# Wider value blocks, split weight rounding in front of the post norms, and a new order in the openings of a three-layer transformer kernel

## Chip, cores and metric

The kernel runs on one core of one Trainium2 chip. The metric is the device time of one execution in microseconds (us). Three runs of the kernel before took 2750.37, 2750.61 and 2752.51 us, median 2750.61 us.

## What is computed

The input is 512 tokens of width 1024. Two "hybrid" layers are followed by a third block of another kind. A hybrid layer is

```python
def hybrid_layer(x, ...):
    h = rms_norm(x, g_mix_pre)
    u = h @ w_in                                   # 1024 -> 3200 columns
    aq, ak, av, cu, rq, rk, rv, rg = jnp.split(u, SPLITS, axis=-1)
    y_att = chunk_attention(aq, ak, av, rel_bias)  # 6 heads of 64
    y_conv = conv_module(cu, ...)                  # 31 taps, width 256
    y_ret = retention(rq, rk, rv, rg)              # 6 heads of 64
    mix = jnp.concatenate([y_att, y_conv, y_ret], axis=-1) @ w_out
    x = x + rms_norm(mix, g_mix_post)
    h = rms_norm(x, g_mlp_pre)
    f = jnp.square(jax.nn.relu(h @ w_up)) @ w_down # 1024 -> 4096 -> 1024
    return x + rms_norm(f, g_mlp_post)
```

`av` and `rv`, the values of the attention and of the retention, are 384 columns each. The third block (a gated MLP, a state space scan, two attentions, gates, a second gated MLP) begins with an RMS norm of the same kind.

## The kernel before

**Products in three passes.** Every weight and every activation of a product is split into a rounded tile (`w_hi`, `h_hi`) and a rest (`w_lo`, `h_lo`), and TensorE (PE) computes hi x hi, hi x lo and lo x hi into the same PSUM bank. Activations lie with features on the partitions: 8 tiles (`KD = 8`) of 128 x 512. The weights come in a list of pieces (`layer_pieces`, 50 for each layer), each at most 8 x 256 columns, in two slots that alternate. SyncE loads a piece into `w_raw`; ScalarE (ACT) rounds it in `round_block` (L347); VectorE (DVE) subtracts in `rest_block` (L356); PE multiplies in `product` (L387). The rounding of piece n + 2 waits until PE has finished piece n, since it overwrites that piece's `w_hi`.

**Kinds of piece.** A "feat" piece of 256 columns is two output tiles of 128 features x 512 tokens: 2 x 8 x 3 matmuls with 512 moving columns. A "tok" piece gives four tiles with tokens on the partitions; its moving operand is the weight, so each of its 4 x 8 x 3 matmuls streams as many columns as the piece is wide. The 14 pieces of `w_in` (`N_IN = 14`) are: 0 and 1 the convolution's input; 2 to 4 the attention's queries and keys; 5 and 6 its values, tok, 256 and 128 columns; 7 to 9 the retention's queries and keys; 10 and 11 its values, tok, 256 and 128 columns; 12 and 13 its gates. Then follow 4 pieces of `w_out` and 32 of the MLP.

**Attention between the products.** The 24 attention steps (head, query tile) run in slots inside pieces 8 to 13: at a slot PE makes the scores of step i (L725), turns the probabilities of step i - 2 (L736) and mixes step i - 3 with the values (L746); DVE adds the bias and takes the maximum (L1183 to L1197), ACT takes the exponential (L976) and copies the turned probabilities (L985). A feat tile of 24 matmuls has two slots, a tok tile one (`slots_of`). Six rotary steps (L717, L1149 to L1153) lie in every second slot from piece 10 on. After the attends of a piece, DVE's order has `rest_block` of the piece two further on.

**Post norm and opening.** At the end of the mixing part and of the MLP the output is normed and added to x. ACT squares the output tiles (L1060, L431); GpSimd (POOL) adds squares 1 to 5 to square 0 (`squares_added`, L453); PE sums over the partitions with a matrix of ones (`added_total`: L458 for the added tile, L436 for tiles 6 and 7, two passes each); ACT takes logarithm and exponential (`norm_rooted`, L476, L478). In `post_norm_dve` DVE scales output tile k (L487), makes the `h_lo` of tile k - 1 (L513) and adds tile k to x (L524). In `split_x` ACT makes `h_hi` of tile k from x (L508) and then the square of x (L532), and POOL adds those squares as well (L453). The next norm's root is applied later, to the products' outputs, so PE can begin on unnormed x: `opening` runs the next two pieces tile by tile in the order `OPENING`: tiles 0 to 4 of both pieces, tiles 5 to 7 of the first, the sum of squares, tiles 5 and 6 of the second, a "turn" of the root where the next layer needs one (L466), tile 7 of the second. For each tile k it waits for `h_lo` and issues, for either output tile, hi x hi (L561), hi x lo (L562), lo x hi (L563). There are six openings: the first one of the kernel (order `FIRST_OPENING`), one in front of the MLP of either layer, one at the end of either layer, and one in front of the third block's second MLP.

The rounding and the rest of the second opening piece stand, on ACT and DVE, between the last output tile and the post norm:

```python
                    act.activation(sq_f[:, k, :], tile_of(b, m), ACT.Square).then_inc(S["squares"], 1)
                    act.activation(out_sb[:, k, :], tile_of(b, m), ACT.Copy).then_inc(S["g_free"], 1)
                round_block(act, b.n + 2)
            norm_rooted(act, N0 + 1)
```

## Time and profile before

| | us |
|---|---|
| median of the runs | 2750.61 |
| the profiled execution: its own time | 2752.54 |
| its span in the trace | 2750.7 |
| PE busy in the span | 2640.1 (96%) |
| DVE busy | 1333.4 (48%) |
| ACT busy | 943.5 (34%) |
| POOL busy | 426.2 (15%) |
| mean granted clock of PE | 0.985 of full |

The chain of work that ended last is to 87% PE, to 72% the matmuls of `product`. Busy time of an engine is the union of its instructions; matmuls overlap, so their pace is read from the distance of their starts. The profiled execution took 1.93 us more than the median run, and 1.8 us of its time lie outside the span.

### The profile page before, as it was taken

Reading aid. Unit: us, or ns where it says so; the run is one execution under the profiler, and the core shown is the slowest. Engines: PE = TensorE matmul, PEld = TensorE weight load, DVE = VectorE, ACT = ScalarE, POOL = GpSimd, SP = SyncE. Lnnn points to the kernel's source line nnn. Section 1 sums busy time; section 2 is a strip of 40 time slices with the busy share of each in tenths; the row PEclk is TensorE's granted clock in tenths of the full one; section 3 lists DMA queues with packets and bytes.
Section 4 is the critical chain, followed back from the end, with each engine's and each line's share of the span. In section 5 each row is a group of like instructions: output and inputs, shape, how many; then the busy total and the mean of one; then the engine's idle time right before and its main releaser. Section 6 shows DMA issues by size and latency. Waiting matters only on the chain.

```text
span 2750.7 us, 31141 instructions
## 1 busy us (share of the span) xinstructions
PE 2640.1 (96%) x12096; PEld 2083.9 (76%) x12096; DVE 1333.4 (48%) x1649; ACT 943.5 (34%) x1340; POOL 426.2 (15%) x375
## 2 busy tenths in 40 slices
PE   8999899999999989999899999899999997999998
PEld 6875688887876668888688888777776675788886
DVE  6744542334854463243544332597864456443432
ACT  4333442332333443232332232432344453322221
POOL 2101100001110110000211101186620320111100
PEclk9999999999999999999999999999999998999999
DMA  3310222222220112223132223411231033222222
GB/s 140 134 39 31 72 97 100 99 92 92 100 85 31 60 65 105 92 92 107 61 107 91 98 101 108 150 62 61 73 107 66 16 106 140 77 104 94 84 94 82
DMA packets 41001, 241.75 MB, mean 88 GB/s; under 512 B 4800, under 2 KB 5312, under 8 KB 17984
## 3 DMA queue, kind: packets, MB, share of 16 engines
q1 hardware_dynamic: 40624, 239.24, 24.7%
q8 instruction: 73, 1.20, 0.2%
q0 software_dynamic: 272, 1.05, 0.1%
q14 instruction: 32, 0.26, 0.0%
HBM read 231.88 MB, written 8.39 MB: 87 GB/s over the span
## 4 chain that ended last, share of the span: by engine, by line
PE 87%; DVE 6%; ACT 4%; issue 2%; DMA 0%; DVEq 0%; SPq 0%; ACTq 0%
PE gemm L387 72%; ACT w_hi L347 2%; DVE x_sb L524 2%; PE score L725 1%; PE mixed L746 1%; DVE w_lo L356 1%; DVE h_lo L513 1%; PE mixed L1569 1%; PE gemm L561 1%; ACT h_hi L508 1%; PE score L1558 1%; PE gemm L562 1%; PE gemm L563 1%; PE mixed L436 1%; PE turned L736 1%
## 5 line engine op out<-in xcount | busy, mean ns | idle before, releaser
L356 DVE TENSOR_TENSOR w_lo<-w_raw,w_hi 128x2048 fp32r<-128x2048 f32 (+3 forms) x225 | 474.3, 2108 | 698.1 <-ACT w_hi L347 697.9
L387 PE MATMUL gemm<-h_hi,w_hi 128*128 128x512 f32 x1744 | 693.8, 398 | 7.6 <-DVE w_lo L356 7.2
L387 PE MATMUL gemm<-h_hi,w_lo 128*128 128x512 f32 x1744 | 681.1, 391 | 0.0
L387 PE MATMUL gemm<-h_lo,w_hi 128*128 128x512 f32 x1744 | 680.5, 390 | 0.0
L347 ACT ACTIVATE w_hi<-w_raw 128x2048 fp32r<-128x2048 f32 (+3 forms) x225 | 393.4, 1749 | 450.4 <-PE gemm L387 398.8
L387 PEld LDWEIGHTS gemm<-h_hi,w_hi 128*128 128x128 f32 x1744 | 328.6, 188 | 78.8 <-DVE w_lo L356 8.2
L387 PEld LDWEIGHTS gemm<-h_hi,w_lo 128*128 128x128 f32 x1744 | 328.2, 188 | 69.7
L387 PEld LDWEIGHTS gemm<-h_lo,w_hi 128*128 128x128 f32 x1744 | 328.7, 188 | 66.0 <-issue 1.7
L387 PE MATMUL gemm<-f_hi,w_hi 128*128 128x512 f32 x512 | 199.2, 389 | 0.0
L387 PE MATMUL gemm<-f_lo,w_hi 128*128 128x512 f32 x512 | 199.2, 389 | 0.0
L387 PE MATMUL gemm<-f_hi,w_lo 128*128 128x512 f32 x512 | 199.2, 389 | 0.0
L453 POOL TENSOR_TENSOR sq_f<-sq_f 128x512 f32<-128x512 f32 x30 | 47.7, 1589 | 742.0 <-ACT sq_f L431 648.1
L387 PE MATMUL gemm<-g_hi,w_hi 128*128 128x512 f32 x352 | 137.1, 390 | 0.0
L387 PE MATMUL gemm<-g_lo,w_hi 128*128 128x512 f32 x352 | 136.9, 389 | 0.0
L387 PE MATMUL gemm<-g_hi,w_lo 128*128 128x512 f32 x352 | 136.9, 389 | 0.0
L561 PE MATMUL gemm<-h_hi,w_hi 128*128 128x512 f32 x192 | 83.0, 432 | 43.2 <-issue 20.5
L1717 POOL TENSOR_TENSOR swi<-swi,rs 128x512 f32<-128x512 f32 x44 | 56.9, 1295 | 404.6 <-ACT swi L1825 404.6
L387 PEld LDWEIGHTS gemm<-f_hi,w_lo 128*128 128x128 f32 x512 | 96.1, 188 | 20.1
L387 PEld LDWEIGHTS gemm<-f_lo,w_hi 128*128 128x128 f32 x512 | 96.1, 188 | 19.9
L387 PEld LDWEIGHTS gemm<-f_hi,w_hi 128*128 128x128 f32 x512 | 96.1, 188 | 19.8
L387 PE MATMUL gemm<-w_hi,h_hi 128*128 128x256 f32 (+1 forms) x352 | 107.5, 305 | 0.0
L1072 ACT ACTIVATE tt<-tt 128x512 f32<-128x512 f32 x64 | 40.3, 632 | 194.1 <-DVE tt L1276 194.1
(379 smaller groups left out, 3888.2 us busy)
## 6 DMA issues: line engine op xcount, KB each, us to landing
w_raw<-in_w SPq DMA_DIRECT2D x171, 1024.0 KB, 4.7
w_raw<-in_w SPq DMA_DIRECT2D x16, 768.0 KB, 4.0
w_raw<-in_w SPq DMA_DIRECT2D x16, 640.0 KB, 3.7
w_raw<-in_w SPq DMA_DIRECT2D x18, 512.0 KB, 3.5
bias_t<-in_att_bias SPq DMA_DIRECT2D x2, 1536.0 KB, 8.8
decay_t<-in_c_decay SPq DMA_DIRECT2D x2, 1536.0 KB, 8.0
x_sb<-in_x SPq DMA_DIRECT2D x4, 512.0 KB, 6.5
x_kept<-x_sb SPq DMA_DIRECT2D x1, 2048.0 KB, 10.8
```

The source lines that it names most:

```text
L347: act.activation(w_hi[:, b.slot, 0:size], w_raw[:, b.slot, 0:size], ACT.Copy).then_inc(S["w_rounded"], 1)
L356: dve.tensor_tensor(w_lo[:, b.slot, 0:size], w_raw[:, b.slot, 0:size], w_hi[:, b.slot, 0:size].bitcast(F32), ALU.subtract).then_inc(S["w_r ...
L387: mm = pe.matmul(dst, lhs, rhs, start=b.first and k == 0 and j == 0, stop=b.last and k == b.kt - 1 and j == 2)
L436: mm = pe.matmul(o_ps[:, 0:n], ones[:], sq[:, k, :], start=k == 0, stop=k == KD - 1)
L453: pool.tensor_tensor(sq[:, 0, :], sq[:, 0, :], sq[:, k, :], ALU.add).then_inc(S["sq_added"], 1)
L508: act.activation(h_hi[:, k, :], x_sb[:, k, :], ACT.Copy, scale=gain[:, k:k + 1]).then_inc(S["norm_hi"], 1)
L513: dve.scalar_tensor_tensor(out=h_lo[:, k, :], in0=x_sb[:, k, :], scalar=gain[:, k:k + 1], in1=h_hi[:, k, :].bitcast(F32), op0=ALU.mult, op ...
L524: dve.tensor_tensor(x_sb[:, k, :], x_sb[:, k, :], out_sb[:, k, :], ALU.add).then_inc(S["x_done"], 1)
L561: pe.matmul(dst, wh[:, k, c], h_hi[:, k, :], start=k == 0, stop=False)
L562: pe.matmul(dst, wh[:, k, c], h_lo[:, k, :], start=False, stop=False)
L1072: act.activation(tt[:, 2 * j + m, :], tt[:, 2 * j + m, :], ACT.Square).then_inc(S["f_sq"], 1)
L1717: pool.tensor_tensor(swi[:, m, :], swi[:, m, :], rs[:], ALU.mult).then_inc(S["silu_r"], 1)
```

## The change

- The values of attention and retention are laid side by side in the weights (`in_columns`) and cut into three tok pieces of 256 columns: pieces 5 and 6, and piece 10. A layer has 13 pieces of `w_in` and 49 in all. The values lie in one buffer `values`; the last tile of `ret_sq` gets a place of its own. Every tok tile now has two slots, one halfway through its 24 matmuls and one behind them, so the number of slots stays 22.
- In front of the post norms the second opening piece is rounded and its rest taken in two halves of 128 columns of each tile (`round_half`, `rest_half`). The first half is done while PE computes the last output tile. At the end of the mixing part ACT's order is square 7, second half, root, copy of tile 7; DVE waits for that copy before the post norm. At the end of the MLP the squares of tiles 6 and 7 come ahead of the halves.
- The squares of x in the four openings behind a post norm are added by DVE inside `post_norm_dve`, one after each addition to x, and no longer by POOL.
- Everywhere one more square (tile 6) is added before the sum, so `added_total` has one tile fewer for PE.
- In `opening`, PE waits for `h_hi` of tile k, issues hi x hi and lo x hi (of both pieces where they stand together in the order), and then waits for `h_lo` and issues hi x lo.

```diff
-    feat(3 * a, 3 * a + 2 * CONV_W)
-    feat(0, 2 * a)
-    tok(2 * a, 3 * a)
-    r = 3 * a + 2 * CONV_W
-    feat(r, r + 2 * RET_W)
-    tok(r + 2 * RET_W, r + 3 * RET_W)
-    feat(r + 3 * RET_W, r + 4 * RET_W)
+    feat(0, 2 * CONV_W)
+    feat(QK_AT, QK_AT + 2 * a)
+    tok(VALUES_AT, VALUES_AT + 2 * WCOLS)
+    feat(RQK_AT, RQK_AT + 2 * RET_W)
+    tok(VALUES_AT + 2 * WCOLS, VALUES_AT + 3 * WCOLS)
+    feat(RG_AT, RG_AT + RET_W)
...
+        def round_half(act, n, m):
+
+            b = plan[n]
+            if m == 0:
+                act.wait_ge(w_in_s[b.slot], ONCE.loads(n))
+            act.wait_ge(S["units"], plan[n - 2].u0 + m + 1)
+            act.activation(half_of(w_hi, b, m), half_of(w_raw, b, m),
+                           ACT.Copy).then_inc(S["w_rounded"] if m else S["half_rounded"], 1)
+
+        def rest_half(dve, n, m, halves):
+
+            b = plan[n]
+            if m:
+                dve.wait_ge(S["w_rounded"], n + 1)
+            else:
+                dve.wait_ge(S["half_rounded"], halves)
+            dve.tensor_tensor(half_of(w_lo, b, m), half_of(w_raw, b, m), half_of(w_hi, b, m).bitcast(F32),
+                              ALU.subtract).then_inc(S["w_rest"] if m else S["half_rest"], 1)
...
-            for k in range(1, KD - 2):
+            for k in range(1, KD - 1):
...
-            for k in (KD - 2, KD - 1):
-                norm_add(pe, i, sq, k)
+            norm_add(pe, i, sq, KD - 1)
...
+            def add_square(k):
+
+                base = added_by(i + 1) - (KD - 2)
+                dve.wait_ge(S["squares"], KD * i + k + 1)
+                if k > 1:
+                    dve.wait_ge(S["sq_added"], base + k - 1)
+                dve.tensor_tensor(sq[:, 0, :], sq[:, 0, :], sq[:, k, :], ALU.add).then_inc(S["sq_added"], 1)
 
             for k in range(KD):
                 norm_scale(dve, i, k, out_sb, out_sb, gain)
@@ -522,6 +569,8 @@
                     raw_rest(dve, j, k - 1, next_gain)
                 dve.wait_ge(S["normed"], normed + k + 1)
                 dve.tensor_tensor(x_sb[:, k, :], x_sb[:, k, :], out_sb[:, k, :], ALU.add).then_inc(S["x_done"], 1)
+                if k > 1:
+                    add_square(k - 1)
             raw_rest(dve, j, KD - 1, next_gain)
...
-                    if k >= waited:
-                        pe.wait_ge(S["h_ready"], ready + k + 1)
-                        waited = k + 1
+                    pe.wait_ge(S["norm_hi"], ready + k + 1)
...
                         pe.matmul(dst, wh[:, k, c], h_hi[:, k, :], start=k == 0, stop=False)
-                        pe.matmul(dst, wh[:, k, c], h_lo[:, k, :], start=False, stop=False)
-                        mm = pe.matmul(dst, wl[:, k, c], h_hi[:, k, :], start=False, stop=k == KD - 1)
-                        if k == KD - 1:
-                            mm.then_inc(S["units"], 1)
+                        pe.matmul(dst, wl[:, k, c], h_hi[:, k, :], start=False, stop=False)
+                    held.append(b)
+                    if n + 1 < len(order) and order[n + 1] == (1 - at[0], k):
+                        continue
+                    pe.wait_ge(S["h_ready"], ready + k + 1)
+                    for b in held:
+                        wh = view(w_hi, b)
+                        for m in range(b.tiles):
+                            mm = pe.matmul(bank[b.bank + m][:], wh[:, k, m * P:(m + 1) * P], h_lo[:, k, :],
+                                           start=False, stop=k == KD - 1)
+                            if k == KD - 1:
+                                mm.then_inc(S["units"], 1)
+                    held = []
...
             squares_added(pool, N0 + 1, sq_f)
-            squares_added(pool, N0 + 2, out_sb)
             squares_added(pool, N0 + 3, sq_f)
-            squares_added(pool, N0 + 4, sq_f)
...
                     for m in range(b.tiles):
+                        softmax(slot0[b.i] + 2 * m)
                         if m % 2:
                             for q in (m - 1, m):
-                                evacuate_one(b, q, rv[:, q, cols])
-                        softmax(slot0[b.i] + m)
+                                evacuate_one(b, q, values[:, 2, q, :])
+                        softmax(slot0[b.i] + 2 * m + 1)
...
+                    if k == KD - 1:
+                        round_half(act, b.n + 2, 1)
+                        norm_rooted(act, N0 + 1)
                     act.activation(out_sb[:, k, :], tile_of(b, m), ACT.Copy).then_inc(S["g_free"], 1)
-                round_block(act, b.n + 2)
-            norm_rooted(act, N0 + 1)
+                    if k == KD - 2:
+                        round_half(act, b.n + 2, 0)
+                if b.i < W_OUT + 3:
+                    round_block(act, b.n + 2)
...
-            norm_squares(act, N0 + 3, out_sb, sq_f, wait=(S["g_free"], last_down), tiles=(KD - 2, KD - 1))
+            for m in range(2):
+                norm_squares(act, N0 + 3, out_sb, sq_f, wait=(S["g_free"], last_down), tiles=(KD - 2 + m,))
+                round_half(act, plan1[DOWN[1] + 7].n + 2, m)
             norm_rooted(act, N0 + 3)
...
+            for m in range(2):
+                rest_half(dve, plan1[W_OUT + 3].n + 2, m, 2 * lay + 1)
+            dve.wait_ge(S["g_free"], plan1[UP[0]].t0)
+            post_norm_dve(dve, N0 + 1, gains["mix_post"], cnt("normed", 0), J0 + 2, gains["mlp_pre"], out_sb)
```

## Rows read from the trace of the kernel before

**Rows 1.** The page: busy us of each engine, share of the span, instructions.
```profile
PE 2640.1 (96%) x12096; PEld 2083.9 (76%) x12096; DVE 1333.4 (48%) x1649; ACT 943.5 (34%) x1340; POOL 426.2 (15%) x375
```

**Rows 2.** Windows, instructions of L387 alone: both value pieces of the attention, layer 0.
```profile
72.55:84.06 11.51, 11.51 (x97) 11.51 (x96) 1.00 0.42 153
84.06:94.74 10.68, 10.68 (x99) 10.68 (x97) 1.00 0.58 225
```

**Rows 3.** Windows, all engines: the two value pieces of the retention, layer 0.
```profile
143.84:165.28 21.44, 21.44 (x140) 16.71 (x139) 10.15 (x25) 7.14 (x18) 0.27 (x1) 1.00 0.08 25
165.28:185.78 20.50, 20.50 (x140) 16.02 (x139) 11.12 (x25) 6.96 (x17) 0.00 (x0) 1.00 0.15 52
```

**Rows 4.** Chain of work, 143 to 170 us: start us, us, what.
```profile
160.51 3.05 PE gemm L387 x24
...
165.34 2.83 PE gemm L387 x24
```

**Rows 5.** Timeline of DVE, 143 to 154 us.
```profile
146.72 1.22 DVE L356 TENSOR_TENSOR w_lo<-w_raw,w_hi 128x1024 fp32r<-128x1024 f32 x1 [1.77 <-ACT w_hi L347]
147.87 0.28 DVE L1183 SCALAR_TENSOR_TENSOR probs<-score,bias_t 128x128 f32<-128x128 f32 x1
```

**Rows 6.** Timeline of ACT, 144 to 150 us.
```profile
145.65 1.04 ACT L347 ACTIVATE w_hi<-w_raw 128x1024 fp32r<-128x1024 f32 x1
```

**Rows 7.** Timeline of ACT, 305.7 to 312.5 us (end of the output projection).
```profile
305.78 0.60 ACT L1060 ACTIVATE sq_f<-gemm 128x512 f32<-128x512 f32 x1 [4.35 <-PE gemm L387]
306.27 0.59 ACT L1061 ACTIVATE out_sb<-gemm 128x512 f32<-128x512 f32 x1
306.75 1.91 ACT L347 ACTIVATE w_hi<-w_raw 128x2048 fp32r<-128x2048 f32 x1
308.55 0.69 ACT L476 ACTIVATE rs<-mixed,eps_c 128x512 f32<-128x512 f32 x1
309.27 0.63 ACT L478 ACTIVATE rs<-rs 128x512 f32<-128x512 f32 x1
```

**Rows 8.** Timeline of DVE, 305.7 to 322 us (post norm in front of the MLP).
```profile
310.90 0.74 DVE L487 SCALAR_TENSOR_TENSOR out_sb<-out_sb,par_sb,rs 128x512 f32<-128x512 f32 x1
...
313.83 0.68 DVE L524 TENSOR_TENSOR x_sb<-x_sb,out_sb 128x512 f32<-128x512 f32 x1
...
315.30 0.75 DVE L513 SCALAR_TENSOR_TENSOR h_lo<-x_sb,par_sb,h_hi 128x512 fp32r<-128x512 f32 x1
315.97 1.77 DVE L524 TENSOR_TENSOR x_sb<-x_sb,out_sb 128x512 f32<-128x512 f32 x1
```

**Rows 9.** Timeline of POOL, 311 to 322 us.
```profile
315.86 1.33 POOL L453 TENSOR_TENSOR out_sb<-out_sb 128x512 f32<-128x512 f32 x1 [18.99 <-ACT out_sb L532]
```

**Rows 10.** Chain of work, 290 to 350 us.
```profile
312.40 0.73 ACT h_hi L508
...
333.65 0.76 DVE h_lo L513
...
336.96 1.72 PE mixed L436 x4
...
342.79 7.25 PE gemm L387 x32
```

**Rows 11.** Windows, all engines: stretches of three openings (the granted clock behind the busy times).
```profile
308.30:314.00 5.70, 0.01 (x1) 0.02 (x1) 5.15 (x6) 2.81 (x5) 0.00 (x0) 0.71 0.31 92
314.00:317.50 3.50, 3.49 (x8) 2.79 (x9) 3.37 (x4) 1.24 (x2) 1.33 (x1) 0.50 0.38 157
...
2373.90:2377.60 3.70, 0.01 (x1) 0.00 (x0) 3.00 (x3) 0.74 (x2) 0.00 (x0) 1.00 0.00 0
```

**Rows 12.** Chain of work, 669 to 712 us (end of layer 0).
```profile
669.28 1.91 ACT w_hi L347
...
675.17 0.76 DVE out_sb L487
...
708.25 3.85 PE gemm L387 x17
```

More of the change, by code:

```diff
@@ L598, in slots_of @@
         def slots_of(b):
-            return 2 * b.tiles if b.kind == "feat" else b.tiles
+            return 2 * b.tiles
         slot0 = {b.i: sum(slots_of(c) for c in plan[SOFT_AT:b.i]) for b in plan[SOFT_AT:N_IN]}
@@ L779, in layer_tensor @@
                     product(pe, b, h_hi, h_lo, halfway=lambda m: attend(slot0[b.i] + 2 * m), between=after)
-                else:
-                    product(pe, b, h_hi, h_lo, between=lambda m: attend(slot0[b.i] + m))
                 if b.i == MEAN_AT:
@@ L916, in layer_gpsimd @@
             by_root(plan1[9], [rqk[:, 4 + m, :] for m in range(2)])
-            for b in plan1[12:14]:
-                by_root(b, [rg[:, 2 * (b.i - 12) + m, :] for m in range(b.tiles)])
+            for b in plan1[11:13]:
+                by_root(b, [rg[:, 2 * (b.i - 11) + m, :] for m in range(b.tiles)])
             pool.wait_ge(S["ln_done"], cnt("ln_done", 2))
```

69 lines of the change are left out of this document (42 added, 27 removed).

## The prediction

> **What bounds the kernel now.** I read the page first, then PE's idle gaps in the timeline, then the chain of waits and the windows of the stages that the change touches. PE is busy for 96% of the span [rows 1], so time can only come from two places: matmuls that go away or run at a worse pace than they need, and the few places where PE waits. The change works on one of each.
>
> The first is the value pieces. A tok tile streams the weights, so a piece of 128 columns needs as many matmuls as one of 256. The reader is to see that it is hardly quicker: 96 matmuls take 11.51 us at 256 columns, 0.120 us each, and 10.68 us at 128, 0.111 us each [rows 2]. In the retention's pieces, runs of 24 take 3.05 and 2.83 us [rows 4].
>
> The second is the openings behind a post norm. PE waits 5.7 us for the first tile [rows 11], works through the early tiles, and in the end waits for the last `h_lo`, ready at 334.4, before it can finish at 342.8 [rows 10]. DVE feeds it too slowly, and the rows show why: the addition to x takes 0.68 us while POOL rests and 1.77 us while POOL adds squares [rows 8, 9]; POOL's add begins 0.11 us ahead of DVE's. Five of the eight additions are of the slow kind. A tile then takes 1.77 - 0.08 (the overlap of neighbours) + 0.73 of ACT [rows 10] + 0.75 of DVE + handoffs, 3.24 us, where PE needs only 12 matmuls of 7.25/32 = 0.227 us [rows 10], 2.72 us.
>
> **Value pieces.** Removed for each layer: two pieces of 128 columns, 10.68 + 4 x 2.83 = 22.0 us. Added: one of 256, 11.51 us if it lies alone. The second half of piece 6 lies outside the attention, the third piece inside it, so I take piece by piece: pieces 5 and 6 go from 22.19 to 23.02 us (+0.8), and the retention's loses 4 x 2.83 = 11.3. Net -10.5 us. The attention's own matmuls stay, as does the number of slots.
>
> What this uncovers: the pieces 10 and 11 took 41.9 us for eight slots, 5.2 us each [rows 3]; now it is (41.9 - 11.3)/8 = 3.8 us. DVE has 21.3 us of work in them, less than the 30.6 that are left, so on average it keeps up. The critical place is the start of the piece. There ACT rounds and DVE takes the rest of the piece two further on, and this is now a wide one: 1.91 and 2.29 us (the wide rest is twice the 1.22 less a fixed part) instead of 1.04 and 1.22 [rows 5 to 7]. DVE's first pass over the scores slips from 147.87 to 149.9, while PE, with 12 matmuls of 0.127 us in front of a slot, is at its second slot at 149.2 (143.8, twice 12 matmuls of 3.05/24, and between them a slot's attention, on average (41.9 - 12.2 - 11.3)/8 = 2.3) and waits there for DVE to free the score bank and then for ACT's copy. A walk through the steps of the piece with the durations of the trace gives 1.5 us, once, and then DVE catches up. Bounds: nothing, and 1.5 us at each of the four tiles, 6.0. I take 1.5: -9.0 us a layer, **-18.0 us**. DMA: one load fewer and the same bytes; the loads run a piece ahead. The convolution's taps on DVE, which PE waits for behind piece 7, are spread over pieces 1 to 6 and get 0.8 us more.
>
> A rule that speaks against this part stands in the Trainium skill, TensorE: Matmul & The Clock Gate, section Back-to-back issue gap: the isolated distance of two matmuls grows with the streamed columns, N/2.4 + 2.5 ns. By it two narrow matmuls cost 112 ns and a wide one 109, and the part would gain 0.3 us a layer before the stall. The rows go against it: 0.111 and 0.120 us.
>
> **Start of the post norm.** In front of the MLP ACT does square 0.60, copy 0.59, rounding 1.91, logarithm 0.69, exponential 0.63, and DVE's rest ends only at 310.9 [rows 7, 8]. After: square (to 306.4), half a rounding (1.04 as in rows 6, to 307.3) beside PE's sum, which has two passes fewer (4 take 1.72 us [rows 10]) and ends at 307.5; logarithm, exponential, copy to 309.4; DVE's half rest (1.22) ends at 308.6 and hides. The first scaling starts at 309.4 instead of 310.9: 1.5 us. The first halves (1.04 and 1.22) lie under PE's last output tile of 5.4 us. At the end of a layer the whole rounding stands ahead of both squares [rows 12]. After: output tile 0.7, square 0.6, two passes 1.0, logarithm and exponential 1.35, so 673.0 instead of 675.2: 2.1 us.
>
> **The opening itself.** DVE per tile: addition 0.61, addition of a square 0.61, scaling 0.66, `h_lo` 0.67 as distances of starts (0.08 less than each duration [rows 8]), 2.56 us, with ACT's 0.73 hidden under the second and third. That is quicker than PE's 2.72, so DVE's work stops being the bound and PE becomes it. PE starts with `h_hi` at 309.4 + 0.74 + 0.69 + 0.72 + handoffs = 311.7. Its work: 96 matmuls x 0.227 = 21.8, the sum 1.7 instead of 2.6, and what the low clock costs. Before, PE ran 3.5 us at half clock [rows 11]; at half speed this costs 1.8 us, hidden while DVE was the bound. It is now in the open; PE rests less (4.2 instead of 5.7 us) but begins in what was the low stretch, so I take 2.0 us, with bounds of 0 and 2.9. End: 311.7 + 21.8 + 1.7 + 2.0 = 337.2 instead of 342.8: 5.5 us, twice **-11.0**. At the end of layer 0: 673.0 + 2.2 + 21.8 + 1.7 + 1.0 (the turn) + 2.0 = 701.8 instead of 708.25 [rows 12]: 6.4; at the end of layer 1, the same without the turn, 6.3: **-12.7**.
>
> What is late next: ACT's rounding of the third piece starts when the first piece's tile 7 is done, 5.8 us before the end, and with its rest takes 4.25; it stays hidden by 1.6 us. The new wait of DVE for the last copy holds only `post_norm_dve`, and is priced above.
>
> **The other openings and sums.** The first opening saves two passes, 0.9, but POOL's sixth addition (1.3) falls on DVE's rest of piece 1, for which PE waits: 0, bounds -0.9 and +1.3. The opening in front of the last MLP saves 0.9, but (0, 0)'s hi x lo moves behind the gap of 3.7 us that ends with piece 1: +0.45. There the clock was full behind 3.7 us of rest [rows 11]; 4.2 us may drop it, so again 0, bounds -0.5 and +2. The sum for the state space part gives 0.9, the last one 0.1: **-1.0**.
>
> **Sum.** -18.0 - 11.0 - 12.7 - 1.0 = -42.7 us. Against the profiled execution's 2752.54 this is 2709.8; it stood 1.9 us above the median of 2750.61, so I predict 2708.
>
> **Rivals.**
> - *Feed still too slow.* DVE keeps the old 3.24 us a tile, since each added square waits for ACT or stalls DVE like POOL did. For: DVE is near PE's pace (2.56 against 2.72). Against: without POOL the same addition takes 0.68 [rows 8]. Then an opening gains its earlier start and the shorter sum only, 2.4 in front of an MLP and 3.0 behind it, 10.8 instead of 23.7: 2721. Chance 0.11.
> - *Attention becomes the bound.* The retention's value piece keeps the 41.9 us of pieces 10 and 11, since eight slots cannot follow faster than ACT and DVE pass a step on. Against: DVE's 21.3 us and ACT's 14.1 in 41.9 [rows 3]. Layers then lose 0.8 instead of gaining 9.0: 2708 + 19.7 = 2728. Chance 0.08.
> - *Pace by columns.* A wide matmul costs as much as two narrow ones, 0.222 us: 21.3 against 21.4 us, no gain from the value pieces, 2726. Chance 0.01, as rows 2 speak against it: 0.120 us. The Trainium skill, TensorE: Matmul & The Clock Gate, section Back-to-back issue gap, is the rule by which it would come out so.
> - *The openings don't change.* DVE's wait for the copy behind the root, and `h_lo` at the end of each tile, hold PE as long as the old order did: only pieces and small sums are left, 2750.6 - 19.0 = 2732. Chance 0.04.
> - *Slower by PE's clock.* If the clock stays at 1.2 GHz through the openings, each of the 96 matmuls costs 0.2 us more: 19.2 less the 2.0 counted, four times, 69 us: 2777. It decides from 10.7 us lost per opening, which is 23 of its 25 us at the low clock. Against: rows 11 show 3.5 us low, then full. Chance 0.02. The Trainium skill (TensorE: Matmul & The Clock Gate, Part 1: The HAM clock gate) has the clock rise with sustained activity; the rows agree, 0.50 and then full.
> - About nothing gained: 0.02.
>
> **How the numbers follow.** The forecast has 0.72. Its own range: no stall and no clock loss gives 2701 (the feed's last tile then holds PE at 1.2 us less), all upper bounds but the worst stall 2715. To leave no more than 2 in 10 out the range reaches over the first rival: 2701 to 2722. A difference of 0.2% (5.5 us) is what a measurement of this kernel can tell from none. Faster is everything but the last two: 0.96; same 0.02, slower 0.02.
>
> **What would show it.** Right: no L453 beside L524, L524 at 0.69 throughout; PE without gaps from `h_hi` 0 to the end of each opening, some 25.5 us; no 128-column matmuls in L387; PE waiting about 1.5 us at the second slot of piece 10. Wrong: gaps in front of the last tiles of an opening, waits of L725 or L736 throughout piece 10, or a half clock far into the openings.

## The result and the profile after

The changed kernel took 2715.99 us, median of 4 runs (2713.98 to 2717.78), against 2750.49 us for the kernel before on the same chip: ratio 0.9875, 95% interval 0.9861 to 0.9889. A second series of the same kernel, run at the end of the study beside other runs of the kernel before, gave 2713.20 us against 2752.36, ratio 0.9856 (0.9839 to 0.9872). The change gains 34.5 us in the first series and 39.2 in the second; I had forecast 42.7 and 2708 us. The profiled execution of the first series took 2717.78 us, with a span of 2715.9. The traces below are of this one unless I say "second trace".

The page of the changed kernel, engine busy us, share of the span and instructions, answers to [rows 1]:

```profile
PE 2614.2 (96%) x11880; PEld 2063.0 (76%) x11880; DVE 1322.3 (49%) x1675; ACT 942.2 (35%) x1334; POOL 413.0 (15%) x363
```

PE has 216 matmuls fewer: 96 in either layer's value pieces, and two passes in each of twelve sums. DVE has more instructions and POOL fewer, since DVE adds the squares in four openings.

**Value pieces.** Windows of the changed kernel, the matmuls of `product` alone (start and end, us, then PE and PE's weight loads with their counts, clock, DMA share, GB/s), answer to [rows 2]:

```profile
74.38:85.91 11.53, 11.53 (x98) 11.53 (x97) 1.00 0.31 111
85.91:97.44 11.53, 11.53 (x99) 11.53 (x98) 1.00 0.65 250
```

Both pieces now cost the same 11.53 us, 0.120 us for each of 96 matmuls; the narrow one had taken 10.68. In the retention there is one value piece where two were. Behind its start PE stops twice. The timeline of that place (start us, us, engine, line, what, and in brackets the idle time before it and who ended it):

```profile
150.27 2.29 DVE L374 TENSOR_TENSOR w_lo<-w_raw,w_hi 128x2048 fp32r<-128x2048 f32 x1 [2.62 <-ACT w_hi L365]
...
152.48 0.28 DVE L1242 SCALAR_TENSOR_TENSOR probs<-score,bias_t 128x128 f32<-128x128 f32 x1
...
152.82 0.70 PE L781 MATMUL score<-qk 64*128 64x256 f32 x2 [0.60 <-DVE probs L1242]
...
154.14 0.52 PE L792 MATMUL turned<-ident_sb,probs 128*128 128x128 f32 x3 [0.62 <-ACT out_sb L1037]
```

DVE's rest of the piece, now 2.29 us long, stands in front of its pass over the scores. PE first waits 0.60 us for the score bank and then 0.62 us for ACT's copy, 1.2 us together, once in a layer. Then DVE has caught up.

**Openings.** DVE's timeline in the opening in front of layer 0's MLP shows one tile's four operations (start us, us):

```profile
319.10 0.69 DVE L564 TENSOR_TENSOR out_sb<-out_sb 128x512 f32<-128x512 f32 x1
319.70 0.75 DVE L526 SCALAR_TENSOR_TENSOR out_sb<-out_sb,par_sb,rs 128x512 f32<-128x512 f32 x1
320.37 0.75 DVE L552 SCALAR_TENSOR_TENSOR h_lo<-x_sb,par_sb,h_hi 128x512 fp32r<-128x512 f32 x1
321.03 0.69 DVE L571 TENSOR_TENSOR x_sb<-x_sb,out_sb 128x512 f32<-128x512 f32 x1
321.63 0.69 DVE L564 TENSOR_TENSOR out_sb<-out_sb 128x512 f32<-128x512 f32 x1
```

From one added square (L564) to the next are 2.53 us, where 2.56 were forecast, and the addition to x (L571) takes 0.69 us instead of the 1.77 of [rows 8]. The windows over PE's rests and what follows them (all engines' busy time with counts, granted clock, DMA share, GB/s) answer to [rows 11]:

```profile
303.93:308.17 4.24, 0.00 (x1) 0.03 (x1) 3.20 (x5) 2.62 (x5) 0.00 (x0) 0.98 0.46 149
308.17:311.60 3.43, 3.43 (x9) 2.71 (x10) 3.30 (x6) 1.67 (x3) 0.00 (x0) 0.53 0.29 122
...
957.63:963.30 5.67, 5.67 (x13) 4.44 (x14) 5.54 (x9) 2.92 (x5) 0.00 (x0) 0.50 0.20 81
2336.68:2340.85 4.17, 0.00 (x1) 0.03 (x1) 3.04 (x3) 1.22 (x2) 0.00 (x0) 0.77 0.00 0
2340.85:2345.70 4.85, 4.85 (x12) 3.80 (x13) 2.51 (x3) 2.26 (x4) 1.33 (x1) 0.50 0.61 216
```

The rest in front of the MLP is 4.24 us instead of 5.69. Behind it PE still runs at 1.2 GHz, here for 3.4 us and in layer 1 for the rest of a stretch of 6.8 us. The last two rows are new: the opening of the last MLP, where the kernel before kept 2.4 GHz, now has half the clock for 4.85 us. PE's wait in front of it does not end with the weights of the second piece, whose rest is there at 2340.10, but with DVE's addition to x behind it, which reads the bank that this piece needs:

```profile
2340.02 1.28 DVE L2491 TENSOR_TENSOR x_sb<-x_sb,gemm 128x512 f32<-128x512 f32 x2
```

**The first opening.** DVE's and POOL's timelines, and the windows of PE's wait:

```profile
19.96 3.37 DVE L374 TENSOR_TENSOR w_lo<-w_raw,w_hi 128x2048 fp32r<-128x2048 f32 x1
...
19.63 1.56 POOL L493 TENSOR_TENSOR out_sb<-out_sb 128x512 f32<-128x512 f32 x1
```

```profile
21.00:23.40 2.40, 0.03 (x2) 0.02 (x1) 2.40 (x2) 0.00 (x0) 0.18 (x1) 1.00 0.00 0
23.40:28.20 4.80, 4.80 (x14) 3.84 (x15) 1.26 (x2) 0.00 (x0) 0.00 (x0) 0.64 0.62 218
```

The rest of piece 1 takes 3.37 us beside POOL's sixth addition, where it took 2.28 before. PE stands still for 2.4 us, and 1.3 us after it goes on its clock falls to half for 3.4 us (24.66 to 28.08 us). Before, PE had no gap here.

**Where the time went.** The table is worked out from the starts of PE's instructions at fixed places of the program, in us. Stages that the table leaves out agree within 0.2 us.

| stage | before | after | second trace | difference | forecast |
|---|---|---|---|---|---|
| start to piece 5 of layer 0 | 72.55 | 74.38 | 73.20 | +1.8 / +0.7 | 0 |
| pieces 5 to 9, each layer | 71.29 | 72.16 | 72.16 | +0.9 | +0.8 |
| piece 10 to the retention's scores, each layer | 74.50 | 65.23 | 65.23 | -9.3 | -9.8 |
| retention to the norm's sum, layer 0 (not changed) | 87.24 | 90.19 | 88.59 | +2.9 / +1.3 | 0 |
| sum to first down projection, layer 0 | 102.32 | 96.63 | 97.70 | -5.7 / -4.6 | -5.5 |
| the same, layer 1 | 102.32 | 97.80 | 97.96 | -4.5 / -4.4 | -5.5 |
| last sum to the next piece 5, layer 0 | 71.71 | 65.58 | 66.20 | -6.1 / -5.5 | -6.4 |
| last sum to the next down projection, layer 1 | 255.46 | 250.00 | 250.11 | -5.5 / -5.4 | -6.3 |
| scan to the gated unit (not changed) | 445.35 | 442.60 | 442.42 | -2.8 / -2.9 | 0 |
| gated unit to the last MLP's down projection | 392.27 | 394.21 | 391.28 | +1.9 / -1.0 | 0 |

With -0.2 in front of the scan, the two columns of differences come to -34.9 and -38.8 us. The spans of the traces differ by 34.8 and 38.6 us, the medians by 34.5 and 39.2.

### The profile page after: what moved, and what is told of

Same layout as the page of the kernel before. It is cut to its first block, busy times and chain, and to the rows that moved or that the text cites. A ratio compares the mean times of both kernels' runs of the same rounds, so it can differ in the third digit from the quotient of the medians.

```text
span 2715.9 us, 30733 instructions
## 1 busy us (share of the span) xinstructions
PE 2614.2 (96%) x11880; PEld 2063.0 (76%) x11880; DVE 1322.3 (49%) x1675; ACT 942.2 (35%) x1334; POOL 413.0 (15%) x363
## 4 chain that ended last, share of the span: by engine, by line
PE 88%; DVE 5%; ACT 4%; issue 2%; POOL 1%; DMA 0%; DVEq 0%; SPq 0%; ACTq 0%; POOLq 0%
PE gemm L427 71%; PE gemm L608 2%; PE gemm L609 2%; PE gemm L617 2%; ACT w_hi L365 1%; PE score L781 1%; PE mixed L802 1%; DVE w_lo L374 1%; PE mixed L1635 1%; PE turned L792 1%; PE score L1624 1%; PE score L1679 1%; PE gemm L1738 1%; PE turned L1693 1%; DMA w_raw<-in_w 0%
## 5 line engine op out<-in xcount | busy, mean ns | idle before, releaser
L374 DVE TENSOR_TENSOR w_lo<-w_raw,w_hi 128x2048 fp32r<-128x2048 f32 (+3 forms) x219 | 466.2, 2129 | 681.1 <-ACT w_hi L365 680.8
L365 ACT ACTIVATE w_hi<-w_raw 128x2048 fp32r<-128x2048 f32 (+3 forms) x219 | 385.4, 1760 | 441.9 <-PE gemm L427 382.5
L493 POOL TENSOR_TENSOR sq_f<-sq_f 128x512 f32<-128x512 f32 x24 | 39.5, 1648 | 751.0 <-ACT sq_f L471 693.6
L1338 DVE SCALAR_TENSOR_TENSOR tt<-gemm,rs 128x512 f32<-128x512 f32 x64 | 43.7, 687 | 102.8 <-PE gemm L427 102.8
```

Source lines behind the costliest of these rows:

```text
L365: act.activation(w_hi[:, b.slot, 0:size], w_raw[:, b.slot, 0:size], ACT.Copy).then_inc(S["w_rounded"], 1)
L374: dve.tensor_tensor(w_lo[:, b.slot, 0:size], w_raw[:, b.slot, 0:size], w_hi[:, b.slot, 0:size].bitcast(F32), ALU.subtract).then_inc(S["w_r ...
L493: pool.tensor_tensor(sq[:, 0, :], sq[:, 0, :], sq[:, k, :], ALU.add).then_inc(S["sq_added"], 1)
L1338: dve.scalar_tensor_tensor(out=tt[:, 2 * j + m, :], in0=tile_of(b, m), scalar=0.0, in1=rs[:], op0=ALU.max, op1=ALU.mult).then_inc(S["g_fre ...
```

## Experiments

Eleven kernels ran. Each ratio is to the kernel before, run on the same chip in the same series.

### The two parts alone

`values_alone` is the kernel before with the edits to the pieces and their buffers only; `openings_alone` is the changed kernel without them.

```diff
-    tok(2 * a, 3 * a)
+    tok(VALUES_AT, VALUES_AT + 2 * WCOLS)
...
-    tok(r + 2 * RET_W, r + 3 * RET_W)
+    tok(VALUES_AT + 2 * WCOLS, VALUES_AT + 3 * WCOLS)
```

> The kernel before with the value pieces alone: three wide pieces in place of four, openings, norms and sums as they were. My theory: each layer loses the retention's two narrow pieces and gains one wide one inside the attention, with a stall of about 1.5 us at the second slot of it. By the trace of the changed kernel this is 0.8 us up to piece 7 and 9.3 us down from there to the retention's scores, so 17 us in two layers: 2733.5 us. Rival 1, pace by columns: nothing, 2750. Rival 2, the clock gives a part of it back (in the changed kernel the stretches at half clock in layer 0's retention took 3 us more than before): 2736. Both parts of the change are independent if this run and the next together lose as much as the change, 34.5 us, within 3 us.

> The changed kernel with its value pieces as before: four pieces, narrow ones for the retention. All else of the change stands: DVE adds the squares, halves, the early root, the order of the openings, six additions in place of five. My theory: what the trace of the changed kernel shows outside the attention, first opening +1.8, the openings in front of the MLPs -5.7 and -4.5, behind them -6.1 and -5.5, state space -0.2, last sum -0.9, which makes -21 us: 2729.5, with 3 us either way for stretches at half clock that fall elsewhere. Rival, the openings gain what I forecast and the shortfall of the changed kernel lies in how its two parts meet: -24.7, so 2726.

Measured: 2733.20 us (0.9937, 0.9921 to 0.9954) and 2732.36 us (0.9932, 0.9915 to 0.9948), against 2750.75 before: -17.5 and -18.4 us, together -35.9, where the two series of the whole change give -34.5 and -39.2. So the parts are independent as far as 3 us can tell. Pace by columns is ruled out: the value pieces alone gain 17.5 us. In the trace the pieces 5 to 9 take 0.9 us more and the stage from piece 10 to the scores 9.3 us less, in both layers, as in the changed kernel. The openings alone gain less than I had read off the first trace (21), and in the trace the stages of the four openings lose 4.5, 5.4, 5.7 and 6.2 us, 21.8 in all, with the first at +0.4, the end of the last at +1.9, and both layers' retention behind its scores, which no edit touches, at +1.5 each, and the scan at -3.0.

### POOL adds the squares again

```diff
-                if k > 1:
-                    add_square(k - 1)
...
             squares_added(pool, N0 + 1, sq_f)
+            squares_added(pool, N0 + 2, out_sb)
             squares_added(pool, N0 + 3, sq_f)
+            squares_added(pool, N0 + 4, sq_f)
```

> The changed kernel, but POOL adds the squares in the four openings behind a post norm again and DVE doesn't; starts, order of the matmuls and pieces as changed. My theory (DVE's feed was the bound): the additions to x that fall on POOL's take 1.77 us instead of 0.69, a tile takes 3.2 instead of 2.55 us, PE waits in front of the late tiles, and an opening ends 3.1 us later in front of an MLP and 3.4 behind it: 2716 + 13 = 2729. Rival 1, the old order of the matmuls and the late start were the bound and not the feed: within 2 us of 2716. Rival 2, PE waits so much that its clock falls again within the openings: 2735 or more.

Measured: 2727.65 us (0.9907, 0.9890 to 0.9923), 11.7 more than the changed kernel's first series. DVE's and POOL's timelines of this kernel:

```profile
312.51 1.78 DVE L563 TENSOR_TENSOR x_sb<-x_sb,out_sb 128x512 f32<-128x512 f32 x1
...
315.76 1.78 DVE L563 TENSOR_TENSOR x_sb<-x_sb,out_sb 128x512 f32<-128x512 f32 x1
...
312.41 1.33 POOL L493 TENSOR_TENSOR out_sb<-out_sb 128x512 f32<-128x512 f32 x1 [1.91 <-ACT out_sb L571]
```

The addition to x takes 1.78 us again, POOL's begins 0.10 us ahead of it, and a tile takes 315.76 - 312.51 = 3.25 us. From first to last matmul the four openings take 28.65, 29.84, 28.66 and 28.62 us, as in the kernel before (28.39, 29.58, 28.38, 28.37), though they start as early as in the changed kernel. PE now waits 0.74 and 1.56 us in front of two late tiles, where the changed kernel has no gap. So what set the length of an opening was DVE's feed, and the rows show what slowed it: not that POOL had work, but that it ran beside a DVE instruction with two inputs in SBUF. The Trainium skill (SBUF — State Buffer, section Who interferes with whom) says that such an instruction contends with one of GpSimd that reads SBUF, and that issue order decides who blocks; by that rule, the rows agree, 1.78 against 0.69 us.

### The root and the rounding in their old places

```diff
-                        round_half(act, b.n + 2, 1)
-                        norm_rooted(act, N0 + 1)
...
+                round_block(act, b.n + 2)
+            norm_rooted(act, N0 + 1)
```

and the same at the end of a layer, with DVE's rest whole.

> The changed kernel with one part undone: the last piece in front of a post norm is rounded as a whole, in the old places (in front of the logarithm before an MLP, in front of the squares behind it), and DVE's rest is whole. My theory: the first scaling starts 1.5 us later in front of an MLP and 2.1 us behind it, and PE has no slack to take it up: 2716 + 7.2 = 2723. Rival 1, DVE's feed has slack over PE's pace, so a late start is partly made up: 2719. Rival 2, the longer rest (5.8 us instead of 4.2) lengthens the half clock in each opening from 3.4 to 6.8 us where it isn't so already, another 1.7 us in two of four: 2727.

Measured: 2730.92 us (0.9927, 0.9911 to 0.9944), 14.9 more: a miss, twice the forecast. The timeline of the end of layer 0 shows why:

```profile
658.84 1.91 ACT L365 ACTIVATE w_hi<-w_raw 128x2048 fp32r<-128x2048 f32 x1 [7.92 <-PE gemm L405]
660.66 1.13 ACT L449 ACTIVATE sq_f<-out_sb 128x512 f32<-128x512 f32 x2
660.78 2.29 DVE L374 TENSOR_TENSOR w_lo<-w_raw,w_hi 128x2048 fp32r<-128x2048 f32 x1 [1.31 <-ACT w_hi L365]
661.35 2.85 POOL L471 TENSOR_TENSOR sq_f<-sq_f 128x512 f32<-128x512 f32 x1 [6.56 <-ACT sq_f L449]
664.25 2.08 PE L476 MATMUL mixed<-sq_f,ones_sb 128*128 128x512 f32 x2 [5.50 <-POOL sq_f L471]
```

With the whole rounding ahead of both squares, POOL's sixth addition comes behind square 6 and beside DVE's rest, takes 2.85 us instead of 1.3, and PE's sum waits for it; then its four passes run at half the clock (2.08 us for two, against 1.02 in the changed kernel). In front of the MLPs the opening starts 1.4 us later, as forecast, but is 0.6 us shorter in layer 1 (25.48 against 26.09 us). Not DVE's slack is the reason: the stretch at half clock is 6.8 us in both, and more of it now lies in PE's rest, which leaves 4.5 us instead of 5.7 in the opening. Layer 0 follows the same measure: 25.5 us with 4.5 us of half clock here, 24.9 with 3.2 in the first trace of the changed kernel, 26.0 with 5.5 in the second.

`late_root_five` is this kernel with five additions in each sum, as before the change:

```diff
-            for k in range(1, KD - 1):
+            for k in range(1, KD - 2):
...
-            norm_add(pe, i, sq, KD - 1)
+            for k in (KD - 2, KD - 1):
+                norm_add(pe, i, sq, k)
```

> The kernel with the late root (2730.9 us, 15 more than the changed kernel, where I expected 7), and with five additions of squares in place of six in every sum, as before the change: PE takes square 6 itself. My theory: with the whole rounding in front of them both squares come late at the end of a layer, and the sixth addition, 2.85 us beside DVE's rest, lands in the open between the square and PE's sum; with five it is gone, so the end of a layer is 3.5 us shorter less 0.9 for PE's two passes, twice, while the sums elsewhere take 0.9 more: 2730.9 - 5.2 + 2.6 = 2728, and from the last down projection to the next layer it takes 3 us more than in the changed kernel instead of 7. Rival, the late root costs 7 us there whoever adds the square: 2733.

Measured: 2725.01 us (0.9904, 0.9889 to 0.9919). From the first down projection to the next layer's piece 5 it takes 329.5 us, against 333.8 with six additions and 326.7 in the changed kernel (second trace 327.3): 2.8 more, 3 expected. So the sixth addition and the halved rounding aren't two separate gains. At the end of a layer the sixth addition is only free because the halves let the square of tile 6 go ahead of the rounding; without them it costs 4.3 us, the half clock of the sum included.

### The order of the matmuls

```diff
-                        pe.matmul(dst, wl[:, k, c], h_hi[:, k, :], start=False, stop=False)
+                        pe.matmul(dst, wh[:, k, c], h_lo[:, k, :], start=False, stop=False)
+                        mm = pe.matmul(dst, wl[:, k, c], h_hi[:, k, :], start=False, stop=k == KD - 1)
...
```

The wait for `h_lo` stands in front of each tile's matmuls again.

> The changed kernel with the old order of the matmuls in all openings: hi x hi, hi x lo, lo x hi for each tile, and no start before h_lo. My theory: the order lets PE start 0.75 us earlier in the four openings behind a post norm, and in the first; the feed's end changes little, and ahead of the last MLP the six matmuls of (0, 0) lie in front of the wait again (3.7 us as before instead of 4.17), where the clock may stay up: 2716 + 4 x 0.75 + 0.7 - 2.8 (the last MLP's opening) = 2717. Rival 1, the order is what keeps PE fed with every tile, h_lo being late each time: 2722. Rival 2, the order is worth nothing: 2713.

Measured: 2715.19 us (0.9871, 0.9854 to 0.9887), 0.8 below the first series of the changed kernel and 2.0 above the second, so no difference that the medians can tell. The terms are there, though: the four openings start 0.78 us later behind the sum (5.02 us of rest against 4.24), and are 0.2 to 0.7 us shorter than in the second trace. The last MLP's opening takes 28.9 us against 29.4 and 30.0, because (0, 0)'s product with `h_lo` stands in front of the wait again, 3.72 us against 4.17, and only 3.4 us of half clock follow. What the order gains in four openings, 1.4 us by these numbers, the last one gives back in part, and the rest is below what a median tells.

### PE kept busy

```diff
+        FILL = 14
...
+                    kept_busy(pe, plan1[first.i:first.i + 2], FILL)
                     opening(pe, plan1[first.i:first.i + 2], N0 + 2, out_sb, cnt("h_ready", 2 * KD))
...
+            for j in range(n):
+                m = j % b.tiles
+                pe.matmul(bank[b.bank + m][:], view(w_hi, b)[:, j % KD, m * P:(m + 1) * P],
+                          w_hi[:, b.slot, 0:SEQ], start=True, stop=True)
```

> The changed kernel with 14 idle matmuls of 512 columns behind the norm's sum, before each of the four openings that follow a post norm. They multiply weight tiles already rounded into a bank that the opening's first matmul clears, so nothing of the result hangs on them, and at 0.227 us each they lie inside PE's rest of 4.2 us. My theory: the stretches at half clock in the openings come from that rest; without it they go (3.4, 3.4, 6.8 and 6.8 us long, so 10 us at most), but DVE's feed, 2.55 us a tile, holds PE back from 2.72, so an opening gains 1.2 to 2.5 us: 2716 - 7 = 2709, and no stretch at half clock in the four openings. Rival 1, the half clock doesn't come from the rest: stretches stay and the time is 2716. Rival 2, DVE is the bound as soon as the clock is full: 2713, with gaps of PE in front of the tiles.

Measured: 2706.88 us (0.9835, 0.9819 to 0.9852), 9.1 below the first series of the changed kernel and 6.3 below the second. Windows of this kernel, layer 0 in front of the MLP: the last matmuls before the rest and the idle ones, the first 3.4 us of the opening, and all of it:

```profile
297.70:303.10 5.40, 4.36 (x18) 2.99 (x18) 3.49 (x5) 3.55 (x6) 0.00 (x0) 1.00 0.40 118
303.10:306.50 3.40, 3.40 (x15) 2.80 (x16) 3.27 (x6) 1.60 (x4) 0.00 (x0) 1.00 0.29 120
303.10:328.00 24.90, 24.61 (x104) 19.32 (x105) 20.70 (x30) 13.64 (x21) 0.00 (x0) 1.00 0.06 21
```

The idle matmuls leave 1.04 us of rest, and the clock stays at 1.00, in all four openings. Three of them now take 24.01 us and the one with the turn 25.21, against 24.9 to 26.2 and 26.2 to 26.9 in the changed kernel's two traces. So the half clock cost 0.9 to 2.2 us an opening. 0.3 us of PE's wait is left in the middle, the first place where DVE's feed shows. The half clock does come from the rest: with all but 1.04 us of it filled, no opening has any.

### The first opening

`late_rest` lets PE take piece 1's two products with rounded weights before DVE's rest of that piece is there; `five_first` gives square 6 of this sum back to PE.

```diff
-            (1, 0), (1, 1), (0, 6), (0, 7), "sum", (1, 2), (1, 3), (1, 4), "turn", (1, 5), (1, 6), (1, 7)]
+            ("hi", 0), ("hi", 1), (0, 6), (0, 7), ("lo", 0), ("lo", 1), "sum", (1, 2), (1, 3), (1, 4), "turn",
+            (1, 5), (1, 6), (1, 7)]
```

> The changed kernel with another order in the first opening alone: for the first two tiles of piece 1 PE takes both products of the rounded weights first, for which it doesn't need DVE's rest of the piece, and the product with the rest four steps later. My theory (PE waits 2.38 us there, since POOL's sixth addition stretches DVE's rest from 2.29 to 3.37 us and PE comes 1.2 us earlier than before): the wait goes but for about 0.3 us, and the half clock behind it (24.7 to 28.1 us, 1.7 us lost) too: 2716 - 3.8 = 2712. Rival 1, the half clock is due in any case: 2714. Rival 2, the wait moves to the last tiles, whose rests DVE makes behind the piece's: 2715.5.

```diff
-            for k in range(1, KD - 1):
+            for k in range(1, KD - 1 if i > 1 else KD - 2):
...
-            norm_add(pe, i, sq, KD - 1)
+            for k in (KD - 2, KD - 1) if i == 1 else (KD - 1,):
+                norm_add(pe, i, sq, k)
```

> The changed kernel with POOL's sixth addition undone in the first opening alone (PE takes square 6 itself there, two passes, 0.43 us each). My theory (the sixth addition lies on DVE's rest of piece 1): the rest takes 2.29 us instead of 3.37, PE's wait for it becomes 1.2 instead of 2.4 us and leaves the clock at full, PE pays 0.86: in the first opening 1.1 + 1.7 - 0.9 = 1.9 us less, 2714. Rival 1, the half clock stays: 2715.8, no change. Rival 2, DVE's rest is slow for another reason (it waits or takes 3.37 with POOL at rest too): 2717.

Measured: 2710.22 us (0.9852, 0.9835 to 0.9868) and 2713.13 us (0.9860, 0.9844 to 0.9875). In `late_rest` PE has no gap in the opening, the clock stays at 1.00, and piece 5 starts at 70.96, 3.4 us earlier than in the first trace of the changed kernel and 2.2 earlier than in the second. DVE's timeline of `five_first`, and the window of PE's wait in it:

```profile
20.00 2.28 DVE L374 TENSOR_TENSOR w_lo<-w_raw,w_hi 128x2048 fp32r<-128x2048 f32 x1
```

```profile
21.14:22.33 1.19, 0.00 (x1) 0.00 (x1) 1.19 (x2) 0.00 (x0) 0.00 (x0) 1.00 0.00 0
22.33:28.50 6.17, 6.17 (x26) 4.96 (x27) 1.27 (x2) 0.34 (x1) 0.00 (x0) 1.00 0.48 170
```

Without POOL's sixth addition the rest takes 2.28 us instead of 3.37, and the wait is 1.19 us instead of 2.4: the cause of the stretched rest is shown. Piece 5 starts 1.9 us earlier than in the first trace, as expected, and 0.7 us earlier than in the second. The medians alone would not settle it: against the second series of the changed kernel `five_first` is level.

### The opening of the last MLP

```diff
-                opening(pe, plan2[up:up + 2], i0, sq, ready)
+                opening(pe, plan2[up:up + 2], i0, sq, ready, LAST_OPENING if name == "ffn2" else OPENING)
...
+        LAST_OPENING = [(0, k) for k in range(5)] + [(1, 0), (1, 1), (0, 5), (0, 6), (0, 7), (1, 2), (1, 3), "sum"] + [
+            (1, k) for k in range(4, KD)]
```

> The changed kernel with another order in the opening of the last MLP alone: five tiles of piece 0, whose inputs have long been there, then two of piece 1, and the sum two tiles later than there. My theory: the wait of 4.17 us for piece 1 (rounding 1.91, rest 2.29) is covered by 30 matmuls of 0.227, 6.8 us, and the stretch at half clock behind it (5.7 us of it inside the opening, 2.4 lost) goes: 2716 - 6.5 = 2709.5. Rival 1, the wait goes and the half clock comes elsewhere: 2712. Rival 2, another wait takes its place (the tiles 6 and 7 of x, POOL's additions, the rounding of the next piece behind a later end of piece 0): 2714 or more.

Measured: 2706.62 us (0.9839, 0.9822 to 0.9855), 9.4 below the first series, 6.6 below the second. A window over the end of the product before and most of the opening:

```profile
2322.00:2347.00 25.00, 25.00 (x112) 20.71 (x111) 11.58 (x11) 8.63 (x11) 4.25 (x3) 1.00 0.24 85
```

PE is busy without a gap and at full clock, now that five tiles of the first piece cover the rounding, the rest and the addition to x. The opening takes 23.30 us instead of 30.0 (second trace 29.4). The wait of 3.7 us in [rows 11] was there in the kernel before as well: six of the eight tiles of x were ready, and the old order went to the second piece after one tile.

### All three edits, and the changed kernel again

> The changed kernel with the three edits together: idle matmuls in PE's rests before the four openings behind a post norm, piece 1's product with its rest taken later in the first opening, five tiles of piece 0 first in the opening of the last MLP. My theory: their gains, read where each acts, add up: in the four openings 5.6 us (0.9, 1.0, 2.1 and 1.7 by the trace of the kernel with idle matmuls), in the first 3.4, in the last 9.1: 2716.0 - 18.1 = 2698, and another 3 less where the stretches at half clock in layer 0's retention fall as in the three kernels just run: 2695. Rival, the half clock that is kept away in the openings comes back in stretches elsewhere: 2704 or more.

> The changed kernel once more, unedited, to see how far two executions of one kernel differ by stretches at half clock, since in the other kernels unchanged stages moved by up to 3 us. My theory: their place isn't fixed by the code alone; a few stretches are 3.4 us long in one profile and 6.8 in another, so that layer 0's retention (from its scores to the sum behind it, 90.2 us in the first profile) comes out at 87 to 89 here as in the other kernels, and the median is within 2 us of 2716.0. Rival: the places are fixed by the code and its times, and every stage repeats within 0.3 us, layer 0's retention at 90.2.

Measured: `combined` takes 2697.16 us (2695.79 to 2701.47), ratio 0.9807, 0.9793 to 0.9820. That is 18.8 us below the changed kernel's first series, 16.0 below the second, and 53 below the kernel before. Against the second series the three edits alone gave 6.3, 3.0 and 6.6, 15.9 together, so there the gains add up; against the first they gave 24.3, which don't. The stages are the better witness: piece 5 of layer 0 starts 3.3 us earlier than in the first trace, the four openings' stages lose 5.7, the last 9.0, 18.0 together, where 18.1 were expected. The rival (the half clock comes back elsewhere) is out: the mean granted clock is 0.990, against 0.983 and 0.984 in the changed kernel. Its page:

```profile
PE 2611.5 (97%) x11936; PEld 2062.1 (77%) x11936; DVE 1323.6 (49%) x1675; ACT 942.3 (35%) x1334; POOL 412.7 (15%) x363
```

The changed kernel again: 2713.20 us, so 0.8 us outside what I had allowed. Windows of the first opening in its trace:

```profile
22.64:23.87 1.23, 0.00 (x1) 0.01 (x1) 1.23 (x2) 0.00 (x0) 0.00 (x0) 1.00 0.00 0
23.87:29.00 5.13, 5.13 (x23) 4.25 (x24) 1.27 (x2) 0.00 (x0) 0.00 (x0) 1.00 0.59 204
```

The same code waits 1.23 us here and keeps its clock, where the first trace shows 2.4 us and half the clock behind it. Everything starts 0.5 us later in this trace, the rest of piece 1 too (20.44 instead of 19.96), so that isn't the cause. But PE's clock rises 5.8 us behind its first matmul, where it rose after 3.4 us in the first trace; PE does the first tiles at half clock for longer, and comes to piece 1 at 22.64 instead of 21.00. The other traces show how this works together with the order of the matmuls and the sixth addition. In the table, the clock's rise is counted from PE's first matmul (matmuls start 0.45 us apart until then and 0.23 us behind it), and the wait is PE's for the rest of piece 1 (us):

| kernel | matmuls | additions | clock rises after | wait |
|---|---|---|---|---|
| before | old order | 5 | 5.5 | none |
| `values_alone` | old order | 5 | 2.9 | 0.54 |
| `late_root_five` | new order | 5 | 4.5 | 0.78 |
| `five_first` | new order | 5 | 3.6 | 1.19 |
| `old_order` | old order | 6 | 4.4 | 1.21 |
| `openings_alone` | new order | 6 | 4.4 | 1.89 |
| changed, second trace | new order | 6 | 5.8 | 1.23 |
| changed, first trace | new order | 6 | 3.4 | 2.38 |

Where the clock rises after 4.4 or 4.5 us, the sixth addition is worth 1.1 us of wait (0.78 to 1.89) and the new order 0.7 (1.21 to 1.89); each us by which the clock rises sooner adds about 0.5. Here half clock followed only the three longest waits of all traces (2.27, 2.38 and 2.44 us, in `pool_adds`, the first trace and `late_root`), and not those of 1.9 us and less.

Layer 0's retention takes 88.59 us, against 90.19 in the first trace and 87.24 in the kernel before. In all fourteen traces of this case it takes 87.2 to 87.4, 88.6 to 88.9 or 90.2 us, and never anything between, with 6.8, 10.2 and 13.7 us of half clock in it: each step is 3.4 us more of it and about 1.5 us dear. Where nothing falls to half clock, the stages repeat: from the first down projection to the norm's sum at the end of the layer it takes 261.12 us in both layers of thirteen traces (in `late_root` PE's wait for POOL lies in it).

## Why the prediction was right, and where it was short

The median of 2716.0 lies in the range of 2701 to 2722, and the mechanisms are the forecast ones; 8 us of the 42.7 are missing in the first pair of traces, 4 in the second. Step by step:

- **Value pieces, -18.0: measured -16.8 in both traces, -17.5 alone.** The wide piece takes 11.53 us (forecast 11.51). The stall is 1.2 us (forecast 1.5), at the slot and for the two reasons named. The stage with the retention's values loses 9.3 us where 9.8 were due. What I had left out is that a run of 12 matmuls between two slots takes 1.61 us and not half of the 3.06 of a run of 24: eight of them cost 0.7 us more, of which the shorter stall gives 0.3 back. The rival that attention becomes the bound is out: 9.3 us gained, not 0. The Trainium skill's formula for the distance of isolated matmuls (TensorE: Matmul & The Clock Gate, section Back-to-back issue gap), by which the part would gain next to nothing, doesn't give the pace here, and `values_alone` says so by a run. The same section says itself that for a stream of weight loads and matmuls the formula comes out too low at few columns; the rows agree, 0.111 us at 128 columns where it gives 0.056.
- **Start of the post norm.** PE's first matmul comes 2.2 us earlier behind the sum in front of an MLP (forecast 2.3) and 2.8 us earlier at the end of a layer (forecast 3.1). I had priced the halves there at 2.1 us, against the old sum. `late_root_five` confirms that: its opening starts 2.0 us later than the changed kernel's. What I had not seen is that the sixth addition, which I priced at PE's two passes saved, hangs on the halves: `late_root` lost 4.3 us a layer by it.
- **The opening itself, 25.5 us: measured 24.9 to 26.2 in front of the MLPs, 25.7 and 25.8 at the end of layer 1.** DVE's 2.53 us a tile and PE as the bound are right, and `pool_adds` shows that the feed had been the bound: it alone brings the old 28.6 us back. The rivals "feed still too slow" and "the openings don't change" are out. The term for the half clock, 2.0 us with bounds of 0 and 2.9, measured 0.9 to 2.2 by `kept_busy`. At full clock an opening takes 24.0 us instead of my 23.5, 0.3 of it a wait of PE. Together the four openings gain 21.8 and 19.8 us, forecast 23.7.
- **The first opening, 0 with an upper bound of +1.3: measured +1.8 and +0.7.** This is the step that failed. I had named the place and the row: POOL's sixth addition on DVE's rest of piece 1. Its price, 1.1 us, is in the bound. But I left out three things. The new order sends PE to piece 1 sooner, by 0.7 us as `old_order` shows. The moment at which the clock rises behind PE's first matmul isn't the same in every execution (3.4 and 5.8 us behind it in the two traces), which moves PE's arrival by another 1.2 us; the trace of the kernel before, with 5.5 us and no wait, was a late case. And behind the wait of 2.4 us the clock fell for 3.4 us, which costs about 1.7 us more. In the second trace that stretch is absent, and 0.5 of its +0.7 us is the later start of everything.
- **The last MLP's opening, 0 with bounds of -0.5 and +2: the opening itself takes +1.9 and +1.3.** The clock did fall behind 4.17 us of rest, as I had written it might; I took 0 out of the bounds, and the measured values lie in their upper half.
- **Small sums, -1.0: -0.2.** Of the 0.9 us in front of the scan 0.2 are left, in both traces. The sum itself is 0.8 us shorter; 0.6 of it is lost behind PE's next long wait, of 6.8 us for a rest of weights, where the half clock lasts 5.2 us (5.3 in the second trace) instead of 4.0.
- **PE's clock as a rival, 2777 us:** out; the longest stretch of half clock in the changed kernel's openings is 6.8 us. My working of when it would decide was wrong: 10.7 us lost on top of the 2.0 counted are 25 us at half clock in an opening of 36, not 23 of 25. And no stall and no clock loss add up to 2700, not 2701. Nothing else hangs on either.
- What no step covers: the retention of layer 0 (+2.9 or +1.3) and the scan (-2.8), stages with unchanged code. They cancel in the first pair and give 1.6 us of gain in the second, where another 2.3 us come between the gated unit and the last opening. The retention and the scan differ by their stretches at half clock. In front of the last opening the second trace has 13.7 us of half clock and the first 17.1, which at half speed is 1.7 us; the other 0.6 I did not trace.

## What to carry to other kernels

Price a wait of TensorE at its length plus the half clock that can follow it, and look first for waits like those here, 2.3 to 5.7 us long: in this kernel idle matmuls in four of them and two better orders were worth 16 to 19 us, about half of what the change itself gained. If part of the inputs of a product are ready, spend them on one block before going to the next; the interleaved order pays only where the inputs arrive one by one. When an addition is moved onto GpSimd, or one more is given to it, look at which two-input VectorE instruction it will run beside and who waits for that one; and undo edits in pairs, since one (the sixth addition) can be free only because of another (the halved rounding).

## What the runs showed of the hardware that I had not expected

- Two executions of one kernel differ by where the half clock falls: the clock's rise 5.8 or 3.4 us behind PE's first matmul made a wait of 1.2 or 2.4 us out of the same code, with 0 or 3.4 us of half clock behind it. Unchanged stages moved by 1.5 or 3.0 us between kernels for this reason. A difference of less than 3 us between two medians here needs the traces to be believed.
- Rests of equal length don't cost the same. Behind 4.24 us the first trace has 3.4 us of half clock in layer 0 and 6.8 in layer 1, and the kernel before kept its clock behind 3.72 us in front of the last MLP, while `old_order` lost it for 3.4 us behind the same 3.72 us, and the changed kernel behind 3.75 us at the end of each layer.
- VectorE's subtraction of 128 x 2048 with both inputs in SBUF took 3.37 us beside a GpSimd addition that had begun 0.33 us ahead of it, and 2.28 us alone; the GpSimd addition took 2.85 us where the subtraction had begun 0.57 us ahead, and 1.3 us alone. The one that begins second pays, by a little less than the other has left (1.1 of 1.2 us, and 1.55 of 1.7).
